# Key norm of the RWKV block: summed with the tokens in partitions, root and reciprocal on eight columns, spread back by four products

## The reference, cut to what matters

```python
heads = lambda t: t.reshape(B, T, H, N).astype(f32)        # H = 16 heads, N = 64
kk = heads(k * k_k)
kk = kk / jnp.maximum(jnp.sqrt(jnp.sum(kk * kk, -1, keepdims=True)), 1e-12)
```

## Time and profile before

| what | value |
|---|---|
| median of 3 runs | 1547.41 us (1546.41 to 1547.94) |
| profiled execution, its time | 1550.36 us |
| profiled execution, its span | 1548.4 us |
| busy: TensorE, VectorE, ScalarE, GpSimd | 1424.4 (92% of the span), 925.5 (60%), 636.0 (41%), 78.7 us (5%) |
| mean granted TensorE clock | 0.957 |

### The profile page before, as it was taken

The page is one execution under the profiler, slowest core; times in us unless marked ns, Lnnn a source line. Parts: engine busy times, 40 slices in busy tenths (PEclk is TensorE's granted clock), DMA queues, the critical chain, the costliest instruction groups (busy, mean ns, idle before and its releaser), DMA issues.

```text
span 1548.4 us, 21677 instructions
## 1 busy us (share of the span) xinstructions
PE 1424.4 (92%) x9280; PEld 1273.7 (82%) x9280; DVE 925.5 (60%) x1333; ACT 636.0 (41%) x899; POOL 78.7 (5%) x44
## 2 busy tenths in 40 slices
PE   7999799897899999899989999799988888799997
PEld 4676699896799998776679999698978887699996
DVE  4267744755554445655374444698998765465554
ACT  1342242344344334444354333543335545554443
POOL 0001300001200001200020000100000000000000
PEclk9999799898899999999999999998999999999999
DMA  9422000001475553723156565364544443355551
GB/s 285 136 72 82 28 1 1 1 1 59 132 238 174 194 183 109 245 83 108 55 166 213 173 195 179 122 191 137 163 137 136 137 136 109 109 165 189 186 195 68
DMA packets 154383, 204.96 MB, mean 132 GB/s; under 512 B 7440, under 2 KB 128400, under 8 KB 154160
## 3 DMA queue, kind: packets, MB, share of 16 engines
q1 hardware_dynamic: 154288, 203.59, 40.5%
HBM read 202.53 MB, written 1.05 MB: 131 GB/s over the span
## 4 chain that ended last, share of the span: by engine, by line
PE 69%; DVE 21%; ACT 5%; DMA 3%; issue 2%; DVEq 0%; SPq 0%; ACTq 0%
PE PS L468 16%; PE PS L469 15%; PE PS L470 15%; DVE PH L1952 6%; DVE WL L1539 5%; PE PS L754 3%; PE PS L741 3%; PE PS L758 2%; PE PS L709 2%; PE PS L659 2%; ACT WH L1080 2%; DMA RG<-in_ffn_w_in 1%; PE PS L604 1%; PE PS L560 1%; PE PS L624 1%
## 5 line engine op out<-in xcount | busy, mean ns | idle before, releaser
L1539 DVE TENSOR_TENSOR WL<-RG,WH 128x2048 fp32r<-128x2048 f32 x163 | 372.6, 2290 | 243.0 <-ACT WH L1080 243.0
L468 PE MATMUL PS<-AH,WH 128*128 128x256 f32 x1664 | 480.6, 289 | 13.5 <-DVE AL L1566 9.2
L469 PE MATMUL PS<-AL,WH 128*128 128x256 f32 x1664 | 475.6, 286 | 0.0
L470 PE MATMUL PS<-AH,WL 128*128 128x256 f32 x1664 | 475.2, 286 | 0.0
L1080 ACT ACTIVATE WH<-RG 128x2048 fp32r<-128x2048 f32 x164 | 311.9, 1907 | 130.3 <-PE PS L470 86.5
L468 PEld LDWEIGHTS PS<-AH,WH 128*128 128x128 f32 x1664 | 324.1, 195 | 21.2 <-issue 11.6
L469 PEld LDWEIGHTS PS<-AL,WH 128*128 128x128 f32 x1664 | 324.3, 195 | 1.7 <-issue 0.2
L470 PEld LDWEIGHTS PS<-AH,WL 128*128 128x128 f32 x1664 | 324.1, 195 | 0.0
L468 PE MATMUL PS<-WH,HH 128*128 128x512 f32 x304 | 118.7, 390 | 0.0
L469 PE MATMUL PS<-WL,HH 128*128 128x512 f32 x304 | 118.7, 390 | 0.0
L470 PE MATMUL PS<-WH,HL 128*128 128x512 f32 x304 | 118.3, 389 | 0.0
(11 more groups left out here) (274 smaller groups left out, 1845.1 us busy)
## 6 DMA issues: line engine op xcount, KB each, us to landing
RG<-in_ffn_w_in SPq DMA_DIRECT2D x44, 1024.0 KB, 5.1
RG<-in_w_ff SPq DMA_DIRECT2D x32, 1024.0 KB, 5.3
RG<-in_w_in SPq DMA_DIRECT2D x30, 1024.0 KB, 5.2
RG<-in_ffn_w_down SPq DMA_DIRECT2D x22, 1024.0 KB, 4.9
RG<-in_moba_w_qkv SPq DMA_DIRECT2D x12, 1024.0 KB, 5.9
RG<-in_w_rkv SPq DMA_DIRECT2D x7, 1024.0 KB, 5.3
PA<-in_w_rkv SPq DMA_DIRECT2D x5, 1024.0 KB, 5.4
RG<-in_w_o SPq DMA_DIRECT2D x4, 1024.0 KB, 6.9
```

The lines of the kernel that those rows point to most:

```text
L468: e.matmul(o, lh, rh, start=start, stop=False)
L469: e.matmul(o, lh, rl, start=False, stop=False)
L470: return e.matmul(o, ll, rh, start=False, stop=stop)
L1539: v.tensor_tensor(WL[:, lo_n % NW, :], ring(SPLIT[lo_n]), WH[:, lo_n % NW, :].bitcast(F32), ALU.subtract).then_inc(s_lo, 1)
```

## The change

For each part, the sum over the head is taken by four products whose stationary operand is a block of the squares and whose moving operand is `sel2` (two columns, one for each head): the result has the tokens in partitions and eight columns (four blocks, two heads). Root, clamp and reciprocal run on these eight columns (`RN`). A copy repeats each column 64 times into `qq`, and four products with the identity turn the four blocks back to channels in partitions, in `PS[6]`, from which `kk` is scaled. TensorE issues these four products after `bonus(j - 1)` and before the projections of the next part; VectorE does its part of the norm ahead of `bonus(j - 1)`.

```diff
@@ vectors and tiles
+        RN = ST[:, 192:200]
@@ tensor_program, for each j
                 e.wait_ge(s_kq, j + 1)
                 if j:
-                    e.wait_ge(s_nr, j)
-                e.matmul(PS[6][:, :], cst('bones'), qq, start=True, stop=True).then_inc(s_nm, 1)
+                    e.wait_ge(s_ks, j)
+                for q in range(4):
+                    t = e.matmul(PS[6][:, 2 * q:2 * q + 2], qq[:, q * 128:q * 128 + 128], cst('sel2'), start=True, stop=True)
+                t.then_inc(s_nm, 1)
                 if j:
                     bonus(j - 1)
+                e.wait_ge(s_nq, j + 1)
+                for q in range(4):
+                    t = e.matmul(PS[6][:, q * 128:q * 128 + 128], qq[:, q * 128:q * 128 + 128],
+                                 ident, start=True, stop=True)
+                t.then_inc(s_nb, 1)
@@ tensor_program, gate products
-                        e.wait_ge(*((s_nr, 4), (s_rs_, 4))[h])
+                        e.wait_ge(*((s_ks, 4), (s_rs_, 4))[h])
@@ scalar_program, for each j
-                s.activation(qq, PS[6][:, :], ACT.Sqrt, bias=0.0, scale=1.0).then_inc(s_nr, 1)
+                s.activation(RN, PS[6][:, 0:8], ACT.Sqrt, bias=0.0, scale=1.0).then_inc(s_nr, 1)
@@ vector_program, for each j
+                v.wait_ge(s_nr, j + 1)
+                own_dve(v.tensor_scalar(RN, RN, 1e-12, None, ALU.max))
+                own_dve.done()
+                own_dve(v.reciprocal(RN, RN))
+                own_dve.done()
+                v.tensor_copy(v3(qq, 64), RN.unsqueeze(2).broadcast_to([128, 8, 64])).then_inc(s_nq, 1)
                 if j:
                     bonus(j - 1)
-                v.wait_ge(s_nr, j + 1)
-                own_dve(v.tensor_scalar(qq, qq, 1e-12, None, ALU.max))
-                own_dve.done()
-                own_dve(v.reciprocal(qq, qq))
-                own_dve.done()
-                own_dve(v.tensor_tensor(kk, kk, qq, ALU.mult))
+                v.wait_ge(s_nb, j + 1)
+                own_dve(v.tensor_tensor(kk, kk, PS[6][:, :], ALU.mult))
```

More of the change, by code:

```diff
@@ L173, in build @@
         s_kr, s_dz, s_dt, s_mid, s_ee = (sem(n) for n in ("kr_mm", "decay_mm", "decay_tanh", "decay_mid", "decay_exp"))
-        s_kq, s_nm, s_nr, s_rs_, s_gr, s_gk = (sem(n) for n in ("k_sq", "k_norm_mm", "k_norm", "r_out", "r_decayed", "k_decayed"))
+        s_kq, s_nm, s_nr, s_nq, s_nb, s_rs_, s_gr, s_gk = (sem(n) for n in ("k_sq", "k_norm_mm", "k_norm", "k_rnorm", "k_rnorm_mm", "r_out", "r_decayed", "k_decayed"))
         s_ks, s_yp, s_bm, s_bv = (sem(n) for n in ("k_scaled", "rk_out", "bonus_mm", "bonus_out"))
```

## The result

The changed kernel takes 1561.16 us (median of 4 runs, 1560.62 to 1564.01) beside 1547.62 us for the kernel before: ratio of the timed runs 1.0083, 95% interval [1.0068, 1.0097]; the medians lie 13.5 us apart. The forecast was 1557.9 us. The profiled execution took 1564.01 us, 13.65 us more than the one before.

What follows compares the result with a forecast made beforehand. Between 54 and 154 us TensorE's loop runs beside a nearly equal ScalarE and VectorE loop. 6.8 + 4.5 + 1.5 - 2.3 = +10.5 us on the profiled 1550.36, adjusted for its 0.2% excess over the median: 1557.9 us, range 1551.0 to 1562.0.

Steps and rivals of the forecast that it cites:

- Mechanism: First three parts: the next projections (14.0 us) stand behind TensorE's wait for VectorE's copy; TensorE alone sets the round, 22.1 us.
- Order, +6.8 us: Three rounds on TensorE: four identity products wait for the copy ahead of the projections; 66.2 instead of 59.4 us.
- The lower bound: VectorE's copy with a repeated column: at least 0.42 us, as a one-input instruction on 512 columns; 0.69 was taken.
- Both falls of the clock: Kernel before, near 91.8 and 112.2 us: head sum and bonus lie in the low stretch, off the path, costing nothing.
- Clock, +4.5 us: First three rounds: TensorE's idle time drops the granted clock to half, slowing the work behind it; 1.5 us a round.
- the sign to look for: Changed trace: granted clock at 0.5 in the first 2 to 3 us of the projections.
- Hold, +1.5 us: VectorE's eight-column clamp may be held by GpSimd's L2107, 0 to 1.0 us a round; half taken over three rounds.
- Last part, -2.3 us: First form product to end of `bonus(3)`: the bonus follows the gates without a wait, ending at 22.0 instead of 24.33.
- the forecast case: Whole kernel: order wait plus falling clock, own range 1554.9 to 1561 us, chance 0.64.
- More is lost: Rival: full holds, 1.8 us for each clock fall and a fall costing the gate products 1.7; +14.6, 1562.0 us, chance 0.08.
- its fall in the gate products: Last part, within a rival: a clock fall that costs 1.7 us in the gate products.
- VectorE's relief decides: Rival: the ScalarE and VectorE loop sets the pace, so lighter VectorE work gains 8 to 10 us, some 1538; chance 0.06.

Runs made afterwards that it cites:

- order alone: Changed kernel, TensorE's wait filled with 16, 12 and 12 unused identity products and ScalarE's receptance copy placed after VectorE's copy: 1554.39 us, ratio 1.0031.
- wait alone: Kernel before, with TensorE made to wait for VectorE's 512-column clamp after the bonus of parts 0 to 2: 1557.05 us, ratio 1.0041.
- without the hold: Changed kernel, ScalarE waiting for VectorE's copy before copying the receptance: 1557.86 us, ratio 1.0051; later use adds the four identity products moved behind eight projection products: 1542.56 us.
- early spread: Changed kernel, the four identity products issued behind the first eight of the next part's 32 projection products: 1542.6 us, ratio 0.9952.
- filled wait: Changed kernel, TensorE multiplying the identity with itself 20, 15 and 15 times while it would wait for the copy: 1554.96 us, ratio 1.0033.

## Why the prediction held, and where it was off

**Mechanism.** It held: the projections stand behind TensorE's wait, and TensorE sets each round. Shown three ways: with the order alone a round takes 21.80 us (22.1 worked out), a wait alone slows the kernel before, and moving the spread by eight products turns the change into a gain.

**Order, +6.8 us.** Measured +5.98 (65.40 - 59.42). Nearly all of the 0.8 between is the copy: 0.43 us and not the 0.69 taken. The lower bound was right: the repeated column does not slow it. The Trainium skill (VectorE: DVE Perf Modes, section "What auto-detection actually checks") has a one-source instruction with both ends in SBUF and an even outer dimension run in a faster mode, and the trace agrees.

One reading was wrong. Both falls of the clock in the kernel before were said to lie off the path, but the second lies on its chain:

```profile
111.99 1.92 PE PS L723 x2
...
139.02 1.05 PE PS L723 x2
```

Head sum and bonus take 1.92 and 1.71 us there, and 1.05 and 0.91 at the full clock (the earlier trace rows has the two of the bonus). So the 59.42 us hold some 1.7 us of low clock, and the 65.40 of the order alone hold none: as an estimate, against rounds without that fall the order costs some 7.7 us, and of the clock's 6.1 us below the kernel before had paid 1.7 already. The sum stays as it is. That the fall cost the stage nothing in the end may still be right, but it was not tried: VectorE is busy or waits for ScalarE's exponentials until 130.54, and could not have begun its masks (130.58) earlier.

**Clock, +4.5 us.** The fall came in all three rounds, and the term was too small. Against the order alone, spread and projections took 1.7, 1.4 and 3.0 us more on the chain (2.08 + 14.64, 2.08 + 14.33 and 2.08 + 15.86 against 1.16 + 13.82): +6.1. In the second execution of the changed kernel, from the spread's start to the end of the round, it is +5.3, without the hold +6.9. The 1.5 a round assumed that the level returns within some 3.4 us of dense work. It took 3.6, 3.0 and 6.1, and the loss is about half of each; of the projections the first 1.5, 0.9 and 4.0 us ran at half, where 2 to 3 was the sign to look for. That a wait brings a fall was right in all nine waits of these three executions, but it is no law: a wait of 3.65 us passed without one (the wait alone), and two kernels saw falls without a wait.

**Hold, +1.5 us.** Half was the wrong choice between two bounds: the clamp was held in every round, by 0.98 us, +2.9 in all. GpSimd's start at 75.60 came ahead of the clamp's at 75.93, as the working had it (75.7 and 76.0). The Trainium skill (VectorE: DVE Perf Modes, section "Two Vector instructions with no wait between them") says that an instruction in a two-port mode reads through an interface shared with GpSimd; by it the sum would have had 3.0, and the trace is near it with 2.9. Only the clamp was held: GpSimd had finished (77.05) when the copy began (77.34).

**Last part, -2.3 us.** Measured -1.8. The spread took 1.17 and the bonus 1.10 us where 0.91 was taken for each, and the third gate product waited 0.19 us for `s_ks`.

**Sum.** 5.98 + 6.1 + 2.9 - 1.8 = +13.2 us in the profiled executions, and 13.5 between the medians, where +10.5 was forecast. The median of 1561.16 lies inside the stated range, near its upper end, just past the forecast case's own (1561). The clock was put 1.6 us too low and the hold 1.4, the order 0.8 too high, and the last part gained 0.5 less. In its terms the result is nearly the rival "More is lost" without its fall in the gate products (6.8 + 3.0 + 5.4 - 2.3 = 12.9), to which 0.08 was given; the full hold had a row behind it and deserved more.

**The rival on the other side** (VectorE's relief decides) asked for a TensorE round under 18 to 18.6 us. That is stricter than needed. With the early spread TensorE's rounds are 19.3 us, above that bound, and the kernel is faster than the kernel before, whose rounds are 19.8 us on average; coming down to 18.35 and 18.61 in two rounds, without the hold, brought nothing more that the totals show.

## What to carry to other kernels

When a step goes from one engine to another and back, ask on each engine what stands behind the new wait; here 14 us of ready work stood behind a hand-over of 5, and eight of its products moved ahead of the wait repaired it. Where an engine's queue has both ready work and a wait, put as much ready work ahead of the wait as it lasts, and not more: twice as much gave the gain away to the other loop. And a wait on TensorE can be paid twice: in the changed kernel waits of 4.9, 3.9 and 3.9 us cost another 1.7, 1.4 and 3.0 us, since what followed ran at the low level.

## What the runs showed of the hardware that was not expected

- Products of two columns cost the same as products of 128: eight rows of `128x2` in 1.05 us, eight rows of `128x128` in 1.05 to 1.16 us at the full clock. The eight weight loads are the same in both; that they set the time is likely, but was not tried.
- The low level can last long after work is dense again: 6.1 us in the third round of the changed kernel. And it can begin in the midst of work: in the second round with the filled wait, the level fell at about 96.6 us, with TensorE busy before and after.
- An instruction on eight columns was held for as long as GpSimd's instruction lasted (1.14 us, and 3.33 in the earlier trace rows). Who begins first seems to matter: where the clamp on 512 columns and GpSimd's instruction begin together (116.38, the kernel before), it takes 0.42 us; where GpSimd begins first (100.59 and 101.11, the wait alone), 0.95. And not every instruction is held: the wide reciprocal takes 3.35 us at 116.83 too, while GpSimd works until 117.83.
- Fifty products that nobody needs made the changed kernel faster by 0.36 to 0.50%.
